# Spacing the chunks of the activation tiles 1088 instead of 1056 columns apart, in a float32 inference step of a hybrid streaming encoder

## The reference

```
for l in 0, 1:
  hn = rmsnorm(x) * norm_mix_pre[l]
  l = 0: z = hn @ w_in (1024 x 2048), split into u, v, xb, gb
         a = gelu(u) * (masked 128x128 mixing of rmsnorm(gelu(v)) over frames + bias)
         b = RG-LRU(conv4(xb)) * gelu(gb)
         m = concat(a, b) @ w_out
  l = 1: bg, cg, xv = split(hn @ w_in (1024 x 3072));  m = (bg * conv3(cg * xv)) @ w_out
  x = x + rmsnorm(m) * norm_mix_post[l]
  f = relu(rmsnorm(x) * norm_ffn_pre[l] @ up (1024 x 4096))**2 @ down (4096 x 1024)
  x = x + rmsnorm(f) * norm_ffn_post[l]
```

## Time and profile before

| | |
|---|---|
| median of 3 runs | 2244.39 us (2242.55 to 2244.78) |
| the profiled execution, its own time | 2245.18 us |
| its span | 2243.3 us |
| mean granted TensorE clock | 0.992 of full speed |
| PE busy | 2198.3 us, 13,817 matmuls |
| DVE, ACT, POOL busy | 881.6, 668.9, 163.3 us |
| moved by DMA | 143.02 MB, mean 64 GB/s |

### The profile page before, as it was taken

The page is one execution under the profiler, slowest core; times in us unless marked ns, Lnnn a source line. Parts: engine busy times, 40 slices in busy tenths (PEclk is TensorE's granted clock), DMA queues, the critical chain, the costliest instruction groups (busy, mean ns, idle before and its releaser), DMA issues.

```text
span 2243.3 us, 32193 instructions
## 1 busy us (share of the span) xinstructions
PE 2198.3 (98%) x13817; PEld 2182.8 (97%) x13817; DVE 881.6 (39%) x1348; ACT 668.9 (30%) x1141; POOL 163.3 (7%) x156
## 2 busy tenths in 40 slices
PE   8987999999999999999999999999999999999998
PEld 7887999999999999999999999999999999999997
DVE  4576327522332332233663323284223323323335
ACT  5464335510320230233421111354113203202333
POOL 1115300000000000000023323000000000000000
PEclk9998999999999999999999999999999999999999
DMA  6111233211111111114221113131111111111132
GB/s 213 47 29 30 61 102 99 64 48 48 46 43 45 48 48 48 47 48 134 85 69 48 48 48 113 60 116 48 43 44 48 48 48 48 47 48 48 49 124 78
DMA packets 228893, 143.02 MB, mean 64 GB/s; under 512 B 5248, under 2 KB 227408, under 8 KB 228752
## 3 DMA queue, kind: packets, MB, share of 16 engines
q1 hardware_dynamic: 228304, 140.89, 20.7%
q0 software_dynamic: 416, 0.07, 0.0%
q10 hardware_dynamic: 32, 0.01, 0.0%
HBM read 119.22 MB, written 21.73 MB: 63 GB/s over the span
## 4 chain that ended last, share of the span: by engine, by line
PE 94%; DVE 3%; ACT 1%; issue 1%; DMA 0%; DVEq 0%; ACTq 0%
PE ps L708 31%; PE ps L709 30%; PE ps L711 30%; DVE lru L1540 1%; PE ps L795 1%; PE ps L752 1%; PE ps L768 0%; PE ps L820 0%; DVE mixed L1559 0%; PE ps L761 0%; PE ps L833 0%; DVE w_all L1351 0%; ACT L1147 0%; PE ps L806 0%; DMA w_all_raw<-in_w_in_even_dram 0%
## 5 line engine op out<-in xcount | busy, mean ns | idle before, releaser
L708 PE MATMUL ps<-x_hi,w_all 128*128 128x352 f32 x2328 | 765.0, 329 | 6.7 <-DVE xb_pad L1469 4.2
L709 PE MATMUL ps<-x_lo,w_all 128*128 128x352 f32 x2328 | 750.7, 322 | 0.0
L711 PE MATMUL ps<-x_hi,w_all 128*128 128x352 f32 x2312 | 745.2, 322 | 0.0
L708 PE MATMUL ps<-h_hi,w_all 128*128 128x352 f32 x1728 | 559.3, 324 | 0.8 <-DVE h_lo L1607 0.8
L711 PE MATMUL ps<-h_hi,w_all 128*128 128x352 f32 x1728 | 554.2, 321 | 0.0
L709 PE MATMUL ps<-h_lo,w_all 128*128 128x352 f32 x1728 | 554.1, 321 | 0.0
L708 PEld LDWEIGHTS ps<-x_hi,w_all 128*128 128x128 f32 x2328 | 440.4, 189 | 10.4 <-issue 5.2
L709 PEld LDWEIGHTS ps<-x_lo,w_all 128*128 128x128 f32 x2328 | 441.4, 190 | 2.7 <-issue 0.8
L711 PEld LDWEIGHTS ps<-x_hi,w_all 128*128 128x128 f32 x2312 | 436.8, 189 | 0.0
L938 ACT CAST w_all<-w_all_raw 128x1024 fp32r<-128x1024 f32 x169 | 176.9, 1047 | 516.7 <-DMA w_all_raw<-in_mlp_down_dram 319.2
L708 PEld LDWEIGHTS ps<-h_hi,w_all 128*128 128x128 f32 x1728 | 324.2, 188 | 1.1 <-DVE h_lo L1607 1.0
(11 more groups left out here) (209 smaller groups left out, 1527.7 us busy)
## 6 DMA issues: line engine op xcount, KB each, us to landing
w_all_raw<-in_mlp_up_dram SPq DMA_DIRECT2D x60, 512.0 KB, 4.0
w_all_raw<-in_mlp_down_dram SPq DMA_DIRECT2D x60, 512.0 KB, 4.1
x_save<-f SPq DMA_DIRECT2D x12, 1408.0 KB, 6.3
x_old<-x_save SPq DMA_DIRECT2D x12, 1408.0 KB, 11.2
w_all_raw<-in_c_w_in_dram SPq DMA_DIRECT2D x22, 512.0 KB, 3.8
w_all_raw<-in_w_in_even_dram SPq DMA_DIRECT2D x15, 512.0 KB, 3.9
x_rows<-in_x_prompt_dram SPq DMA_DIRECT2D x8, 512.0 KB, 6.8
w_all_raw<-in_w_out_even_dram SPq DMA_DIRECT2D x6, 512.0 KB, 4.3
```

The costliest lines, as they stand in the source:

```text
L708: nc.tensor.matmul(dst, wh, hi, start=(i == 0), stop=False)
L709: nc.tensor.matmul(dst, wh, lo, start=False, stop=False)
L711: last = nc.tensor.matmul(dst, wl, hi, start=False, stop=(i == KC - 1))
```

## The change

The chunks of `x_hi`, `x_lo`, `h_hi`, `h_lo` and of the views laid over them (`x_hi_raw`, `x_old`, `h_hi_raw`, `h_lo_raw`, `mixed`) stand `TS` = 1088 columns apart, 4352 bytes. The 32 columns behind each chunk are not used. `f`, the copies of x in DRAM, `w_all` and `w_s` keep their layout. The four buffers grow by 1024 bytes each. For that `ig1`, 4236 bytes, gives up its own place and lies in `h_lo` behind `v_junk`, in the columns of chunks 2 and 3; DVE waits for `lru_pool` at 12 before it writes chunk 2 of `mixed`. The second mixer's buffers over `h_lo` begin at byte 9216 instead of 8320.

```diff
--- before.py
+++ after.py
@@ -26,6 +26,7 @@
 CC = 3
 NJ = 4
 JW = TT // NJ
+TS = TOK + 32
 NB = 6
 M0, M1 = 6, 7
 
@@ -202,13 +203,13 @@
 
         CH = KC * TOK
         at_x_hi = at_byte[0]
-        x_hi = place("x_hi", [P, CH], F32R)
+        x_hi = place("x_hi", [P, KC * TS], F32R)
         at_x_lo = at_byte[0]
-        x_lo = place("x_lo", [P, CH], F32R)
+        x_lo = place("x_lo", [P, KC * TS], F32R)
         at_h_hi = at_byte[0]
-        h_hi = place("h_hi", [P, CH], F32R)
+        h_hi = place("h_hi", [P, KC * TS], F32R)
         at_h_lo = at_byte[0]
-        h_lo = place("h_lo", [P, CH], F32R)
+        h_lo = place("h_lo", [P, KC * TS], F32R)
         at_f = at_byte[0]
         f = place("f", [P, CH], F32)
         at_w = at_byte[0]
@@ -235,13 +236,12 @@
         row_sq = place("row_sq", [P, 9], F32)
         row_root = place("row_root", [P, 9], F32)
         row_rstd = place("row_rstd", [P, 9], F32)
-        ig1 = place("ig1", [P, LV], F32)
-
-
-        x_hi_raw = place("x_hi_raw", [P, CH], F32, at_x_hi)
-        x_old = place("x_old", [P, CH], F32, at_x_lo)
-        h_hi_raw = place("h_hi_raw", [P, CH], F32, at_h_hi)
-        h_lo_raw = place("h_lo_raw", [P, CH], F32, at_h_lo)
+
+
+        x_hi_raw = place("x_hi_raw", [P, KC * TS], F32, at_x_hi)
+        x_old = place("x_old", [P, KC * TS], F32, at_x_lo)
+        h_hi_raw = place("h_hi_raw", [P, KC * TS], F32, at_h_hi)
+        h_lo_raw = place("h_lo_raw", [P, KC * TS], F32, at_h_lo)
 
         x_rows = place("x_rows", [P, SEQ // P, D], F32, at_h_lo)
         x_rows_s = place("x_rows_s", [DEC, D], F32, at_h_hi)
@@ -257,20 +257,20 @@
         v_gain_bc = place("v_gain_bc", [P, HALF], F32, at_h_lo + 2048)
         v_prod = place("v_prod", [P, SEQ // P, P], F32, at_h_lo + 4096)
         v_junk = place("v_junk", [P, HALF], F32, at_h_lo + 8192)
-        gate_w = place("gate_w", [P, 2, HC, P], F32, at_h_lo + 7 * TOK * 4)
-        mixed = place("mixed", [P, KC, TOK], F32, at_h_lo)
+        gate_w = place("gate_w", [P, 2, HC, P], F32, at_h_lo + 7 * TS * 4)
+        mixed = place("mixed", [P, KC, TS], F32, at_h_lo)
         bias_bc = place("bias_bc", [P, HC, P], F32, at_sq)
         v_tok_s = place("v_tok_s", [DEC, HALF], F32, at_sq + HALF * 4)
         lru_step = LV * 4 + (-LV * 4) % 32
         xc, q, ig0, rc, lru_t = [place(f"lru{i}", [P, LV], F32, at_f + i * lru_step) for i in range(5)]
-        ig = (ig0, ig1)
+        ig = (ig0, place("ig1", [P, LV], F32, at_h_lo + 8192 + HALF * 4))
         at_g = at_f + 5 * lru_step
         gelu = [place(f"gelu{i}", [P, TOK], F32, at_g + i * TOK * 4) for i in range(2)]
         ws_t = place("ws_t", [P, HC, P], F32, at_g + 2 * TOK * 4)
 
         c_step = PB * 4 + (-PB * 4) % 32
         cg, cp, cy = [], [], []
-        for n, at in enumerate((at_h_lo + 8320, at_f)):
+        for n, at in enumerate((at_h_lo + 9216, at_f)):
             for i in range(2):
                 cg.append(place(f"cg{n}{i}", [P, TOK], F32, at + i * TOK * 4))
                 cp.append(place(f"cp{n}{i}", [P, PB], F32, at + 2 * TOK * 4 + i * c_step))
@@ -286,7 +286,8 @@
             return buf[:, :].rearrange("p (k n) -> p k n", k=KC)
 
         def pt(buf, c, t):
-            return buf[:, c * TOK + t * TT:c * TOK + t * TT + TT]
+            c0 = c * (TOK if buf is f else TS) + t * TT
+            return buf[:, c0:c0 + TT]
 
         def part(buf, k0, k1, t, c0=0, c1=TT):
             return tiles3(buf)[:, k0:k1, t * TT + c0:t * TT + c1]
@@ -1590,6 +1591,8 @@
 
             def spatial_bias(n):
                 h, part_no = n // 3, n % 3
+                if n == 6:
+                    dve.wait_ge(lru_pool, 12)
                 dve.wait_ge(b_in, 16)
                 dve.wait_ge(sgu_pe, n + 1)
                 if part_no < 2:
```

## The result

| | before | after |
|---|---|---|
| median (12 runs each) | 2244.35 us (2242.55 to 2245.68) | 2248.28 us (2246.52 to 2249.86) |
| the profiled execution, its own time | 2245.18 us | 2249.09 us |
| its span | 2243.3 us | 2247.3 us |
| sum of all pitches of 140 to 175 ns | 2067.9 us (12,978, mean 159.34 ns) | 2071.3 us (12,976, mean 159.63 ns) |

After / before is 1.0019, 95% interval [1.0011, 1.0027]: 4 us slower. The interval leaves out 1, but the step is inside the 0.2% that the prediction counts as no change. The forecast was 2247.5 us. "Pitch" stays the time from one start of a main matmul to the next, in the trace's nanoseconds; the last row adds up those at the fast clock with nothing in between. They hold 3.4 of the 4.0 us by which the span grew.

What follows compares the result with a forecast made beforehand. PE, busy 98% of the span, was taken to bound the kernel through its matmul pitch. Terms +6.1 - 4.8 + 1.8 = +3.1 us on the profiled 2245.2 gave 2248.3, less 0.8 for the median: 2247.5 us, range 2231 to 2264.

Steps and rivals of the forecast that it cites:

- part 1: Main matmuls on PE, chunks 1088 columns apart: new pitches +6.1 us, slow rhythms gone -4.8, restarts +1.8, sum +3.1 us.
- the minus term: Units at 3.84 and 3.87 us, x slot and behind interruptions: these slow rhythms should go with the alternating stream, -4.8 us.
- The restarts in tile 1: Tile 1 matmuls following a restart behind statistics matmuls: half lock at 166.7 instead of 158.3 ns, +2.9 us, taken as +1.8.
- tile 1 locks: Rival, slower: tile 1 locks at a slow pitch, 2284 us at 166.7 ns throughout or 2255 us at 160.0; chance 0.21.
- (2): ig1 moved into h_lo: DVE's wait for POOL ahead of the seventh spatial bias is covered by the last panel's scan; cost 0.
- (3): DVE, ACT and POOL read and write chunks at new places: cost 0, subtractions into h_lo took 510 to 526 ns throughout.
- (4): Transfers: same number and size, only row starts of x_old and the x and h slots move; 0, with 1 us either side.
- No dependence: Rival: the pitch spread comes from tile borders themselves, so the change does nothing to the pitch; 2244.4 us, chance 0.05.
- Tiles 0 and 2 in the slow rhythm: Rival, slower: tiles 0 and 2 run at 161.1 ns, +9.7 us, 2257 us; chance 0.12.
- Faster in uniform streams: Rival: uniform streams settle lower, tiles 0 and 2 at 158.3 ns (2232.8 us) or tile 1 at 155 (2233 us); chance 0.25.

Runs made afterwards that it cites:

- e4: Kernel before with ig1 moved into h_lo as in the change and w_all 128 bytes further on: 2243.18 us against 2244.44, ratio 0.9994.
- e6: Changed kernel with the hb slot's weights 32 columns further on, so every slot's weights start at a 256-byte block's beginning: 2246.46 us, ratio 1.0010 to before.
- e2: Changed kernel with w_all and everything behind it 128 bytes further on: 2245.18 us against 2244.44 for the kernel before, ratio 1.0004.
- e8: Changed kernel with tiles of 384, 320 and 352 columns and weights of every slot but w_s at byte 128 of a block: 2260.78 us, ratio 1.0074 to before.
- e3: Changed kernel with w_all and what is behind it 64 bytes further on: 2252.60 us, ratio 1.0041 to the kernel before.
- e5: e2 plus weights in the x and ha slots 32 columns further on, so all slots but w_s stand at byte 128: 2239.90 us, ratio 0.9984 to before.
- e9: e5 plus w_s, w_s_raw and xb_pad 128 bytes further on in h_hi: 2239.45 us against 2243.79 for the kernel before, ratio 0.9982.
- e10: Changed kernel with w_all 32 bytes further on: 2261.63 us, ratio 1.0081 to the kernel before.
- e11: Changed kernel with w_all 96 bytes further on: 2252.17 us, ratio 1.0039 to the kernel before.
- e1: Kernel before with only ig1 moved into h_lo and DVE's wait for lru_pool at 12: 2244.64 us against 2244.44, ratio 1.0000.
- e7: Changed kernel with tiles of 384, 320 and 352 columns, all starting at a 256-byte block's beginning like the weights: 2253.08 us, ratio 1.0040 to before.

## Why the prediction was right, and where its reasons were not

**The rhythms (part 1).** A panel was to take 11.480 us and takes 11.48; tiles 0 and 2 were to have an even 160.0 and have 160.03 and 160.04 in the rotating slots; tile 1 was to have 158.3 in the mean and has it wherever it is not locked. Both borders of the old kernel were fair samples, which e4 shows by making them change places. The slow rhythms of 3.84 and 3.87 us are gone from the x slot and from most places behind restarts, as the minus term said: 69 units had a mean pitch of 160.5 to 165 ns before, 12 after. The sum of the pitches grew by 3.4 us where the terms gave +3.1; the median grew by 3.9.

**The restarts in tile 1 (+1.8 us).** The size came out right, by luck: 233 pitches at 166 or 167 ns x 8.4 ns = 2.0 us. The reason failed. The step as it was put: "behind each block's statistics matmuls some 90 matmuls of tile 1 follow a restart", half of which lock. In e6 the same restarts stand at the same places, and all 204 locked pitches of the blocks' starts are gone, because the hb slot's weights no longer stand at place 128. 57 of them are in tile 2, in the hb slot's own units, which the step did not look at. The prediction had said of the weights that the rotating slots are at place 0, and had moved the x slot's; it had not worked out hb's. The starts of the locks, in ns (a star marks a pitch with a restart in it):

```
e2, end of unit 59 (x slot, tile 2), then unit 60 (tile 0):     160 160 161 | 162 164 166 | 167 167 166
after, end of unit 77 (hb slot, tile 1), then unit 78 (tile 1): 160 160 161 | 162 164 166 | 167 167 166
e8, end of unit 68, then unit 69 (tile 2, same weights' place): 692* 245 167 167 | 166 167 167
```

In the first two no restart stands at the start of the lock: the weights jump by 128 bytes while the columns keep their place, and the relation goes from 0 to 128. The traces of the kernel after and of e2, e3, e5, e6 and e9 can be counted for this. A unit enters the relation 128 by a jump of the weights (128 or 64 bytes), with no restart in its first nine pitches, 24 times, and locks every time (at least four of the nine at 166 or 167 ns). It enters it by a jump of the columns at a tile's border, out of the even 160, 724 times, and never locks. Out of the slow rhythm at the relation 0, with its pitches of 165 158 159, the same border locks 5 of 25 times: unit 49 in the kernel after and the four of e3. That is like the case of the earlier trace rows. Not every jump of the weights does it: in e10 and e11 (32 and 96 bytes) the x slot's units of tile 1 run at 158.2 and 158.3 ns.

The third row shows the other way in, behind a restart and with no jump, the one that the prediction had in mind. It is less regular: units 69, 357, 549 and 550 in e8, unit 390 in e2 and e9 but not in e5. A restart can also end a lock, as in unit 81 of the kernel after. The locks before unit 48, where restarts are many, were not followed one by one.

Common to all ways is the relation. Over the kernel after, e2, e3, e5, e6 and e9, 1408 of the 1412 pitches of 166 or 167 ns belong to matmuls whose columns stand 128 bytes from their weights. So the relation 128 has two rhythms, the good one of 158.3 ns and the lock of 166.7, and which one a stretch gets hangs on how it was entered. This much the rival *tile 1 locks* had right: it is the uniform stream at place 128 that can lock.

**The other parts.** (2) Cost 0: e1 has the move and the wait alone, and the ratio is 1.0000. (3) DVE's subtractions take 515 to 527 ns. (4) Transfers show nowhere: DMA has 0% of the chain as in the earlier trace rows.

**The rivals.** *No dependence* is out: e2 swaps the tiles' roles without moving a column, and from e2 to e5 the x slot's units change by moving their weights alone. The prediction cited the Trainium skill, page "SBUF — State Buffer", section "Who interferes with whom", for two independent read ports of TensorE; that is not the whole picture here, since the pitch of the same columns goes from 160.0 to 158.3 or 162.1 ns with the place of the weights. Nor does any steady pitch of 352 columns come near the estimate of 149 ns worked out from the Trainium skill, page "TensorE: Matmul & The Clock Gate", section "Back-to-back issue gap", which gives its formula for an isolated matmul; the lowest steady pitch in these runs, each matmul with its own weight load, is 158.3. *Tile 1 locks* happened in seven units, not throughout. *Tiles 0 and 2 in the slow rhythm* did not happen either, but for the few units counted above. *Faster in uniform streams* did not happen for tiles 0 and 2 because they have the relation 0, which is no faster than the others; it is real for the one relation of 128 bytes, and e5 gets it in two tiles out of three by moving weights.

**The best version** is e5 (or e9): 2239.9 us (2239.5), 0.16% (0.18%) below before, by their ratios. Against the kernel after that is 0.9984 / 1.0019, some 0.35% less. The two ratios come from two sessions, each against the kernel before. The step that e5 adds to the change is to make two tiles out of three meet the weights half a block off, with no jumps of the weights from unit 12 on.

What stays open is the mechanism inside: why 128 bytes help 352 columns by 1.7 ns and harm 384 by 2.5, why a jump of the weights leaves a lock that lasts for a unit and more, and what decides over the early locks, which differ between executions.

## What to carry to other kernels

Where PE is busy throughout, read its pitch from the starts, not from the durations, and compare the rhythms at tile borders: they are small samples of another layout, and here their difference times the count of matmuls, less the slow rhythms, gave the growth to a few tenths of a us (+1.3 us forecast; 3.4 - 2.0 = 1.4 measured, the locks aside). Work out the places of both operands, columns and weights, modulo 256 bytes for every slot in use, and keep the weights' place the same from slot to slot. The one relation that was faster here is also the one that locks, so count the locked pitches before you trust it. A relation that is good at one width has to be measured anew at another.

## What was not expected of the hardware

- The pitch of a 128x128x352 fp32r matmul depends on the place of the weights relative to the columns: 158.3, 160.0 or 162.1 ns steady, 166.7 ns locked (the table in e10 and e11).
- The relation 128 has two rhythms at 352 columns, 158.3 and 166.7 ns, and the lock is memory: entered by a jump of the weights it locked 24 of 24 times, by a jump of the columns out of the even 160 in none of 724, and unit 79 has it or not by what the hb slot's weights did two units before (after against e6). Of the pitches of 166 or 167 ns in six kernels, 1408 of 1412 stand at this relation.
- At the relation 0 the surplus over the columns is 13.0 to 13.5 ns for 320, 352 and 384 columns (e7); at the relation 128 it is 13.2, about 11.7 and 16.0 ns (e8).
